# State space and expert layer kernel: fifteen weighted row additions move from VectorE to TensorE, ten held items move behind the first weighted block

## The chip, the cores and the metric

The kernel runs on one core of one Trainium2 chip. The metric is the device time of one execution in microseconds (us); three runs of the kernel before gave 1796.65, 1800.41 and 1805.96, so the median is 1800.41 us. The core has TensorE (PE in the profile, its weight loads are PEld), VectorE (DVE), ScalarE (ACT), GpSimd (POOL, which here issues the gathers) and SyncE (SP, which issues the block loads), each with its own instruction stream, and 16 DMA engines that all queues share. The engines meet through semaphores alone.

## The reference

One layer of a streaming encoder over 512 prompt rows (four tiles of 128 tokens) and 32 sample rows (tile 4), all in float32:

```
h = x + W_out[ concat( shortconv_group(xn), ssd_group(xn) ) ]      # xn = RMSNorm(x)
h = h + CrossAttn(RMSNorm(h), memory K/V)                          # 4 heads, 256 memory rows
h = h + PEER(RMSNorm(h))                                           # 8 heads, top 16 of 16384 experts
y = RMSNorm(h)

# ssd_group, chunk by chunk: decay matrix, two products, state update
y_diag = einsum('bclsg,bclsgh,bcsghp->bclghp', CB, Lm, xdt)
# PEER, per token: 8 heads x 16 experts
hid = gelu( einsum('td,thkd->thk', xb, u_tab[eidx]) )
out = einsum('thk,thkd->td', gate * hid, v_tab[eidx])
```

The last line is what the change touches: a token's output is a sum of 128 rows of `v_tab`, each times a weight of that token.

## The kernel before

**Tiling.** The five token tiles go in two groups: group 0 is tiles 0 and 1, group 1 is tiles 2, 3 and 4. Group 0 passes all dense stages first (input products, convolutions, the state space chain, attention, the expert queries), then group 1. The experts of tiles 1 and 2 are computed densely: all 128 blocks of 128 experts go through TensorE, `lk(b)` multiplying block b of `u_tab` with the tokens (8 matmuls) and `vd(b)` multiplying the weighted result with block b of `v_tab` (4 matmuls, accumulated over all blocks in PSUM banks 0 to 3). The experts of tiles 0, 3 and 4 are gathered: 18 steps i of 16 rows s, one row per token, 0.52 MB for each (i, s) and table.

**Gathered rows.** `("d", i, s)` is a dot product on VectorE of the gathered row of `u_tab` with the token (L1785). After 16 of them ScalarE computes the Gelu (`("ge", i)`, L1328) and VectorE the weights (L1792). `("v", i, s)` then adds weight times gathered row of `v_tab` to the tile (`scalar_tensor_tensor`, L1806). GpSimd issues the gathers in the order u(i, s), v(i-1, s) into rings of four buffers each; a gather waits until the use four before it is done (`u_used`, `v_added`).

**The order.** `plan()` writes one list, `PLAN`, of all work items. Each engine walks through the same list and issues its own part of each item, in order. In the dense stages of group 1 the items of gathered steps 0 to 5 stand between the dense items, placed by a planner with estimated costs. The state space chain of group 1 (the items `s1`, `s2`, `s2b`, `s3`, `s3b`, `s4` of tiles 2, 3, 4, with `z` and `o` projections between them) is such a stage. In it `s2(t)` is on TensorE eight small matmuls (L949), on ScalarE the Relu of their result (L1246), an Exp (L1249) and a small Exp (L1251). `s3(t)` is a product with the state (L962), one with the decay matrix (L969) and one that updates the state (L975). `s4(t)` normalizes the chunk: Square and Sqrt on ScalarE (L1168, L1169), a scaling on VectorE (L1646) and transposes on TensorE (L851), which VectorE drains (L1429).

**PSUM.** There are eight banks. Every TensorE result of the dense stages is a job, job n uses bank n % 8 and waits until job n-8 has been drained.

**The tail.** Before the block loop 22 `lk` are done ahead, with one-hot matmuls `gb` of tile 2 (L1106) between the first of them. The items that the planner took out of the gathered steps 3 to 6 (`late_slots`) are merged with these: the last 22 with `lk(15)` to `lk(21)`. Then VectorE computes `w(0)` to `w(3)` (the weighted hidden values of a block, two instructions each, L1866 and L1867), and the loop goes `w(b+3)`, some gathered items, `vd(b)`, `lk(b+22)`. A buffer of four blocks holds the `w` results, so `w(b)` waits for `vd(b-4)`. The gathered items left over are spread over the blocks in equal shares, at half the share in the last 22 blocks, where there is no `lk` any more. The result of tile t leaves after the last block.

Of the kernel before, what the change touches and what calls it, by code (L numbers as in the profile page):

```python
# [12 lines left out]
P = 128  # L13
# [78 lines left out]
def dense(g):  # L92
# [28 lines left out]
    s += [("o", g, q, t) for q in range(4) for t in TG[g] if ("o", g, q, t) not in s]  # L121

    s += [("norm", 1, t) for t in TG[g]] + kv[10:12]
    if g == 0:
# [75 lines left out]
def plan():  # L200
# [64 lines left out]
    g0 += [("gb", 2, n - 2), ("gb", 2, n - 1)]  # L265
    out += merged(g0, late_slots[4:-22]) + merged(ahead[15:], late_slots[-22:])

    one, two = slots.index(("d", PH + 1, 0)), slots.index(("d", PH + 3, 0))
    extra = merged([x for pair in range(PH // 2) for x in rt(3, pair)] + soft(3), slots[:one])
    extra += merged(rt(NP, 0) + soft(NP), slots[one:two]) + slots[two:]  # L270
    pace = lambda x: dve_us(x) if x[0] in ("d", "v", "final") else 0.0
    work = lambda b: 2 * min(b, NBLK - HRING) + max(0, b - NBLK + HRING)
    total, used, nlk = sum(pace(x) for x in extra), 0.0, HRING
# [85 lines left out]
JOBS = [j for seg in PLAN for j in jobs_of(seg)]  # L359
SEQN = {k: n for n, (k, _) in enumerate(JOBS)}  # L360
OWNER = dict(JOBS)
ORD = {}
# [52 lines left out]
def build_program(nc, a, o):  # L415
    ctx = ExitStack()
    with ctx:
# [133 lines left out]
        OHF = take_(2 * OH_TOK * 2 * P)  # L551
        OH = [cut(OHF, k * OH_TOK * 2 * P, OH_TOK, 2, P) for k in range(2)] + [ar(off, OH_TOK, 2, P) for off in (10752, 12488, 13512)]
        HID, GH, WT = take_(2, TOPK), take_(2, TOPK), take_(2, TOPK)
        assert g_[0] <= 5960, g_[0]
# [23 lines left out]
        ublk_in, vblk_in = [sem(f"ublk_in{r}") for r in range(SR)], [sem(f"vblk_in{r}") for r in range(SR)]  # L578
        lk_done, h_done, wr_done, vd_done = map(sem, "lk_done h_done wr_done vd_done".split())
        xd_done, oh_done, oh_used, g_out, closed = map(sem, "xd_done oh_done oh_used g_out closed".split())  # L580
        hot_done, tt_done, tt_out, fold_done = map(sem, "hot_done tt_done tt_out fold_done".split())
# [21 lines left out]
        def bank_of(key):  # L603
            return PSB[:, SEQN[key] % NB, :]

# [225 lines left out]
        def _(pe):  # L831
            def open_job(key):
                n = SEQN[key]
                if n >= NB:
                    wait_drained(pe, JOBS[n - NB][0])
                return bank_of(key)
# [237 lines left out]
            def settle():  # L1074


                if not settled:
                    for key, _ in JOBS[-NB:]:
                        wait_drained(pe, key)
                    settled.append(True)  # L1080
# [42 lines left out]
            def vd(b):  # L1123
# [17 lines left out]
            does = {"const": const, "state": state, "turn": turn, "memn": memn, "in": in_, "dt": dt, "z": z, "oc": oc, "kv": kv, "kt": kt,  # L1141
                    "s1": s1, "s2": s2, "s3": s3, "s4": s4, "ho": ho, "o": o_, "q": q_, "a1": a1, "a2p": a2p, "a2": a2, "mo": mo,
                    "sk": sk, "pq": pq, "sc": sc, "lk": lk, "tt": tt, "gb": gb, "vd": vd, "fold": fold}
            for seg in PLAN:
# [5 lines left out]
        def _(act):  # L1150
# [201 lines left out]
            def gb(t, n):  # L1352
# [22 lines left out]
                if at + OH_TOK == CH_TOK and c < NSP:  # L1375
                    if small:
                        act.wait_ge(g_out, k + 1)
                    else:
                        act.wait_ge(ev["A"], ORD[("gb", t, n)] + 1)
                    act.dma_start(spill[:, :, c, :].rearrange("k p x -> p k x"),  # L1380
                                  STG[r].rearrange("p (k i) x -> p k (i x)", i=GRP)).then_inc(gs_out[r], 16)

            def leave(t):
                n = rows(t)
                if t in CLOSED:
                    act.wait_ge(closed, CLOSED.index(t) + 1)
                else:
                    act.wait_ge(v_added, (step_of(t, PH - 1) + 1) * TOPK)
                root_mean_square(("leave", t), XN[0:n, t, :], X[0:n, t, :], n, D)

            for row in SMALL_ROWS[:4]:
# [4 lines left out]
                    "ho": ho, "kt": kt, "q": q_, "a1": a1, "a2p": a2p, "a2": a2, "sk": sk, "pq": pq, "sc": sc,  # L1396
                    "keep_x": keep_x, "sme": soft_exp, "ge": gelu, "lk": lk, "oh": oh, "gb": gb, "leave": leave}
            for seg in PLAN:
# [5 lines left out]
        def _(dve):  # L1404
# [427 lines left out]
            def oh(t, n):  # L1832
                d = DENSE.index(t)
                m, c = d * P // OH_TOK + n, n * OH_TOK
                if n == 0 and d == 0:
                    wait_drained(dve, ("tt", 1))
                if n == 0 and d == 1:
                    dve.wait_ge(tt_out, 1)
# [40 lines left out]
            def final(t):  # L1879
# [7 lines left out]
                    "kt": kt, "s1": s1, "s2": s2, "s3": s3, "s4": s4, "o": residual("o"), "a1": a1, "mo": residual("mo"),  # L1887
                    "rt": route, "smd": soft_sum, "d": dot, "v": weighted, "s2b": s2b, "s3b": s3b, "tt": tt, "fold": fold, "oh": oh, "w": w, "close": close,
                    "final": final}
# [33 lines left out]
```

## Time and profile before

| | |
|---|---|
| median of three runs | 1800.41 us |
| lowest, highest | 1796.65, 1805.96 us |
| the profiled execution | 1802.75 us, of which the span is 1801.0 us |
| PE busy | 1678.7 us (93%) |
| PEld busy | 1247.4 us (69%) |
| DVE busy | 1221.1 us (68%) |
| POOL busy | 705.3 us (39%) |
| ACT busy | 366.4 us (20%) |
| moved by DMA | 552.63 MB, mean 307 GB/s |

All times below are from the start of this span. A TensorE instruction on float32 shows as two records, so "x16" of L865 is one projection of eight matmuls, and "x8" of L1128 is one `vd` of four. The granted TensorE clock has two levels, 2.4 GHz (1.00 in the tables) and 1.2 GHz (0.50); a mean between them says how long either held.

### The profile page before, as it was taken

To read this page: it belongs to the slowest core of one execution; us is meant where nothing else is said; L and a number is where in the kernel's file an instruction comes from. 1 tells how busy PE (TensorE), PEld (TensorE's weight loads), DVE (VectorE), ACT (ScalarE), POOL (GpSimd) and SP (SyncE) were. 2 spreads that over 40 slices of the span, in tenths; PEclk is the share of its full clock that TensorE was granted. 3 is DMA by queue.
4 is the path that set the end of the run, shared out by engine and by line. 5 is a ranking of instruction groups with operands and counts; after the bars stand their busy time and mean duration, and the time that the engine had idled before them with its cause. 6 is when DMAs were issued, how large, how long until landed. Compare 5 with 4: busy or idle time off the path is not lost. (4 is left out here: it accounts for less than half of the span.)

```text
span 1801.0 us, 20020 instructions
## 1 busy us (share of the span) xinstructions
PE 1678.7 (93%) x7088; PEld 1247.4 (69%) x7088; DVE 1221.1 (68%) x2626; ACT 366.4 (20%) x910; POOL 705.3 (39%) x601
## 2 busy tenths in 40 slices
PE   7998999999778888899887999999999999999997
PEld 6887888878655677788885666666666666666633
DVE  2352111799688768898987999777666666666675
ACT  1141123111330244642760001101000000000101
POOL 0000000234134438640765555456544444644542
PEclk9999999999878999899998999999999999999999
DMA  6523434789246959995999999999999999999996
GB/s 195 179 93 117 164 117 141 253 271 352 82 140 211 364 175 363 336 345 169 359 318 380 403 407 409 409 409 409 406 408 408 407 409 410 393 410 410 409 376 260
DMA packets 227983, 552.63 MB, mean 307 GB/s; under 512 B 16989, under 2 KB 114957, under 8 KB 227885
## 3 DMA queue, kind: packets, MB, share of 16 engines
q0 software_dynamic: 82944, 302.03, 43.8%
q1 hardware_dynamic: 122180, 237.78, 36.2%
q10 hardware_dynamic: 22760, 11.55, 2.2%
q8 instruction: 57, 0.93, 0.2%
q14 instruction: 42, 0.34, 0.1%
HBM read 534.22 MB, written 16.42 MB: 306 GB/s over the span
## 5 line engine op out<-in xcount | busy, mean ns | idle before, releaser
L809 POOL DMA_INDIRECT M<-in_u_tab,IDX x288 | 342.1, 1188 | 715.9 <-DVE PEER L1785 345.9
L816 POOL DMA_INDIRECT M<-in_v_tab,IDX x288 | 359.2, 1247 | 352.7 <-DVE X L1806 273.7
L1128 PE MATMUL PSB<-M,HST 128*128 128x512 f32 x1024 | 461.6, 596 | 14.8 <-DVE HST L1867 9.9
L1120 PE MATMUL PSB<-XN,M 128*128 128x256 f32 x2048 | 466.4, 382 | 4.9 <-DMA M<-in_u_blocks 3.9
L1120 PEld LDWEIGHTS PSB<-XN,M 128*128 128x128 f32 x2048 | 391.5, 192 | 104.6 <-issue 55.4
L1785 DVE CUSTOM_DVE_ANT_0 M<-M,XN 128x1024 f32<-128x1024 f32 x288 | 351.4, 1221 | 132.8 <-DMA M<-in_u_tab,IDX 120.1
L1806 DVE SCALAR_TENSOR_TENSOR X<-M,PEER,X 128x1024 f32<-128x1024 f32 x256 | 328.1, 1282 | 98.3 <-DMA M<-in_v_tab,IDX 88.3
L1128 PEld LDWEIGHTS PSB<-M,HST 128*128 128x128 f32 x1024 | 195.0, 191 | 218.4 <-issue 201.6
L858 PE MATMUL PSB<-M 128*128 128x256 f32 (+1 forms) x1408 | 327.8, 393 | 9.2 <-DVE M L1429 6.7
L858 PEld LDWEIGHTS PSB<-M 128*128 128x128 f32 x1408 | 266.0, 190 | 64.0 <-DVE M L1429 7.5
L865 PE MATMUL PSB<-M 128*128 128x256 f32 (+1 forms) x1056 | 247.9, 395 | 4.0 <-DMA M<-in_w_out 1.8
L865 PEld LDWEIGHTS PSB<-M 128*128 128x128 f32 (+1 forms) x1056 | 194.8, 187 | 48.9 <-issue 2.4
L1341 ACT ACTIVATE M<-PSB 128x256 f32<-128x256 f32 x128 | 48.7, 381 | 672.1 <-PE PSB L1120 529.8
L1654 DVE TENSOR_TENSOR X<-PSB,X 128x256 f32<-128x256 f32 (+1 forms) x40 | 16.7, 418 | 69.6 <-PE PSB L865 69.6
L1806 DVE SCALAR_TENSOR_TENSOR XN<-M,PEER,XN 128x1024 f32<-128x1024 f32 x31 | 39.8, 1284 | 20.6 <-DMA M<-in_v_tab,IDX 20.3
L1349 ACT ACTIVATE PEER<-PEER 128x128 f32<-128x128 f32 x152 | 48.0, 390 | 28.2 <-DVE PEER L1852 23.1
L1106 PE MATMUL PSB<-PEER 128*128 128x128 f32 x304 | 43.8, 297 | 5.0 <-ACT PEER L1349 2.8
L1852 DVE TENSOR_TENSOR PEER<-iota,PEER 128x1024 f32<-128x1024 f32 x38 | 46.0, 1220 | 3.2 <-PE PSB L1106 1.7
L1106 PEld LDWEIGHTS PSB<-PEER 128*128 128x128 f32 x304 | 41.0, 209 | 8.2 <-ACT M L1370 3.1
L1866 DVE TENSOR_TENSOR HST<-M 128x176 f32<-128x176 f32 x128 | 43.1, 336 | 1.4 <-PE PSB L1128 1.4
L851 PE MATMUL PSB<-ident,M 128*128 128x128 f32 (+1 forms) x160 | 21.3, 281 | 24.0 <-DVE M L1646 19.8
L1168 ACT ACTIVATE XN<-X 128x1024 f32<-128x1024 f32 (+1 forms) x19 | 20.0, 1050 | 114.6 <-DVE X L1654 69.9
(223 smaller groups left out, 1110.5 us busy)
## 6 DMA issues: line engine op xcount, KB each, us to landing
M<-in_u_blocks SPq DMA_DIRECT2D x128, 512.0 KB
M<-in_v_tab SPq DMA_DIRECT2D x128, 512.0 KB
M<-in_w_in SPq DMA_DIRECT2D x24, 1024.0 KB
M<-in_w_pq SPq DMA_DIRECT2D x16, 1024.0 KB
gate_spill<-M ACTq DMA_DIRECT2D x11, 1024.0 KB, 17.0
M<-gate_spill SPq DMA_DIRECT2D x16, 704.0 KB
M<-in_w_out SPq DMA_DIRECT2D x8, 1024.0 KB
M<-in_w_mq SPq DMA_DIRECT2D x8, 1024.0 KB
```

Of the source, the lines that this page charges most:

```text
L809: pool.indirect_dma_start(out=UA[:, s % RR, :], out_offset=None, in_=utab, in_offset=bass.IndirectOffsetOnAxis(ap=IDX[:, n:n + 1], axis=0) ...
L816: pool.indirect_dma_start(out=VA[:, s % RR, :], out_offset=None, in_=vtab, in_offset=bass.IndirectOffsetOnAxis(ap=IDX[:, n:n + 1], axis=0) ...
L858: last = pe.matmul(b[:, 0:n], w[:, c, half * P:(half + 1) * P], src[:, c, :], start=(c == 0), stop=(c == DC - 1))
L865: last = pe.matmul(b[0:n, 0:BW], lhs(c), w[:, c, :], start=(c == 0), stop=(c == DC - 1))
L1106: last = pe.matmul(bank[:, j * P:(j + 1) * P], hot_buffer(t, n)[:, j, 1, :], hot_buffer(t, n)[:, j, 0, :], start=True, stop=True)
L1120: last = pe.matmul(PSB[:, 4 + b % 2, 0:2 * P], UBLK[:, b % SR, c, :], XN[:, 1:3, c * P:(c + 1) * P], start=(c == 0), stop=(c == DC - 1))
L1128: last = pe.matmul(PSB[:, 2 * t + hf, :], WR[:, b % WRING, t * P:(t + 1) * P], VBLK[:, b % SR, hf * 512:(hf + 1) * 512], start=(b == 0), s ...
L1341: act.activation(HR[:, b % HRING, :], PSB[:, 4 + b % 2, 0:2 * P], ACT.Gelu).then_inc(h_done, 1)
L1349: last = act.activation(first, first, ACT.Copy, scale=TT[:, d, 2, c + j:c + j + 1])
L1785: dve.tensor_tensor_reduce(u, u, XN[:, t, :], 1.0, 0.0, ALU.mult, ALU.add, HID[:, par, s:s + 1]).then_inc(u_used, 1)
L1806: dve.scalar_tensor_tensor(out=acc, in0=row, scalar=w, in1=acc, op0=ALU.mult, op1=ALU.add).then_inc(v_added, 1)
L1852: dve.tensor_tensor(hot, bc(iota[:, :].unsqueeze(1).unsqueeze(1), whole), bc(keys.unsqueeze(3), whole), ALU.is_equal).then_inc(hot_done, 1)
```

## The change

First, in the stretch from `s1` of tile 2 to a new item `("sums",)`, which stands ahead of the attention norms of group 1, the fifteen additions `v` of (0, 10) to (1, 8) leave VectorE. For each of them ScalarE builds a diagonal matrix of the weights (Copy of the identity, scaled by the weight of each partition, into a ring of eight), and TensorE multiplies this diagonal with the gathered row, 512 columns at a time, into PSUM banks 6 and 7, where the fifteen products add up. `sums` on VectorE adds both banks to the tile. In this stretch the other jobs use banks 0 to 5 only. The memory of the diagonals is that of the one-hot matrices, which come into use later.

Second, of the 22 late items that were merged with `lk(15)` to `lk(21)` twelve stay there. The last ten (five `d`, five `v`) go to the front of the gathered items of the block loop.

```
@@ dense(g)
+    s += [("sums",)] * g
     s += [("norm", 1, t) for t in TG[g]] + kv[10:12]
@@ plan()
-    out += merged(g0, late_slots[4:-22]) + merged(ahead[15:], late_slots[-22:])
+    out += merged(g0, late_slots[4:-22]) + merged(ahead[15:], late_slots[-22:-10])
...
+    extra = late_slots[-10:] + extra
@@ after PLAN
+SPAN = range(PLAN.index(("s1", TG[1][0])), PLAN.index(("sums",)) + 1)
+ON_PE = [s[1:] for n, s in enumerate(PLAN) if s[0] == "v" and n in SPAN]
+def banks():
+    at, before, last, turn = {}, {}, {}, 0
+    for n, seg in enumerate(PLAN):
+        for key, _ in jobs_of(seg):
+            if n in SPAN and turn % NB >= NB - 2:
+                turn += NB - turn % NB
+            at[key], before[key] = turn % NB, last.get(turn % NB)
+            last[turn % NB] = key
+            turn += 1
...
@@ TensorE
+            def add(i, s):
+                if (i, s) not in ON_PE:
+                    return
+                n, k = i * TOPK + s, ON_PE.index((i, s))
+                if k == 0:
+                    for key in AHEAD_OF_SUMS:
+                        wait_drained(pe, key)
+                    pe.wait_ge(v_added, n)
+                ring_in(pe, va_in, i, s)
+                pe.wait_ge(diag_done, k + 1)
+                for hf in range(2):
+                    last = pe.matmul(PSB[:, NB - 2 + hf, :], DIAG[k % 8], VA[:, s % RR, hf * 512:(hf + 1) * 512],
+                                     start=(k == 0), stop=(k == len(ON_PE) - 1))
+                last.then_inc(v_added, 1)
@@ ScalarE
+            def add(i, s):
+                if (i, s) not in ON_PE:
+                    return
+                k = ON_PE.index((i, s))
+                act.wait_ge(w_done, i + 1)
+                if k >= 8:
+                    act.wait_ge(v_added, i * TOPK + s - 7)
+                act.activation(DIAG[k % 8], ident[:, :], ACT.Copy, scale=WT[:, i % 2, s:s + 1]).then_inc(diag_done, 1)
@@ VectorE
             def add(i, s):
                 t, par, n = step_tile(i), i % 2, i * TOPK + s
+                if (i, s) in ON_PE:
+                    return
...
+            def sums():
+                dve.wait_ge(v_added, ON_PE[-1][0] * TOPK + ON_PE[-1][1] + 1)
+                for hf in range(2):
+                    x = X[:, 0, hf * 512:(hf + 1) * 512]
+                    last = dve.tensor_tensor(x, PSB[:, NB - 2 + hf, :], x, ALU.add)
+                last.then_inc(sums_out, 1)
+                dve.wait_ge(sums_out, 1)
```

What the new list does to the engines' own orders is seen at three places. The line numbers of the changed kernel differ: its L894, L978, L991 are L865, L949, L962 of before, its L1295 to L1297 are L1249 to L1251, its L1268 is L1222, and its L1932 and L1933 are L1866 and L1867.

TensorE in the chain of group 1, from `s2` of tile 2 (L949) on, before; L865 with 32 rows is `z` of tile 4, L962 to L975 is `s3(2)`:

```order
L949 MATMUL PSB<-EARLY,M 128x128 x8
L865 MATMUL PSB<-M 32x256 x8
L962 MATMUL PSB<-HST,M 128x256 x2
L969 MATMUL PSB<-M 128x64 x8
L975 MATMUL PSB<-M 128x256 x2
```

The same place in the changed kernel, L1176 being a product with a diagonal:

```order
L978 MATMUL PSB<-EARLY,M 128x128 x8
L1176 MATMUL PSB<-M,PEER 128x512 x2
L894 MATMUL PSB<-M 32x256 x8
L991 MATMUL PSB<-HST,M 128x256 x2
L998 MATMUL PSB<-M 128x64 x8
```

One product, that of (0, 10), has come between `s2(2)` and the `z` projection that followed it at once.

ScalarE at the same item and up to the norm of the next chunk, changed kernel, from the Exp of `s2(3)` on (L1436 builds a diagonal, L1268 is the Silu of `z`, L1214 and L1215 are Square and Sqrt of `s4(2)`):

```order
L1295 ACT_TABLE_LOAD
L1295 ACTIVATE M<-M 128x1024
L1297 ACTIVATE EARLY<-EARLY 128x24
L1436 ACTIVATE PEER<-ident,PEER 128x128 x2
L1268 ACT_TABLE_LOAD
L1268 ACTIVATE M<-PSB 32x256
L1214 ACTIVATE M,SS<-M 128x512
L1215 ACT_TABLE_LOAD
L1215 ACTIVATE SS<-SS,EPSC 128x1
```

The two diagonals stand behind both Exps of `s2(3)`, and the Silu of `z`, which waits for TensorE, stands ahead of the norm of `s4(2)` as it did before.

VectorE ahead of `w(0)`, changed kernel (L1840 is the dot product L1785 of before, two records each, and L1863 the addition L1806 of before):

```order
L1840 ISA M,PEER<-M,XN 128x1024
L1840 ISA PEER 128x1
L1863 SCALAR_TENSOR_TENSOR X<-M,PEER,X 128x1024
L1932 TENSOR_TENSOR HST<-M 128x176
L1933 TENSOR_TENSOR HST<-M 128x80
```

Ahead of this place stand five dot products and five additions fewer than before. They come after `w(3)`, and with them in the loop the gathered items of all later blocks move back by up to ten items.

## Rows read from the trace of the kernel before

**Rows 1.** Busy time of each engine by stretch, with clock and DMA share

```profile
core 0: us, PE busy (x) PEld busy (x) DVE busy (x) ACT busy (x) POOL busy (x), PEclk, DMA share, GB/s
472.00:592.00 120.00, 93.00 (x418) 68.83 (x418) 93.58 (x242) 31.11 (x72) 38.94 (x31) 0.84 0.51 171
939.00:975.00 36.00, 22.56 (x92) 18.62 (x90) 21.46 (x27) 2.30 (x6) 22.07 (x20) 0.85 1.02 408
975.00:1715.00 740.00, 739.67 (x2560) 487.60 (x2561) 531.54 (x1048) 55.89 (x133) 387.00 (x343) 1.00 1.02 405
```

**Rows 2.** Timeline of TensorE in the chain: start, us, line, idle before and releaser

```profile
480.52 3.64 PE L865 MATMUL PSB<-M 128*32 128x256 f32 x16
...
488.81 2.94 PE L969 MATMUL PSB<-M 128*128 128x64 f32 x16 [3.58 <-issue]
...
508.35 1.12 PE L851 MATMUL PSB<-ident,M 128*128 128x128 f32 x4 [6.36 <-DVE M L1646]
...
528.21 10.00 PE L865 MATMUL PSB<-M 128*128 128x256 f32 x32
541.25 1.11 PE L851 MATMUL PSB<-ident,M 128*128 128x128 f32 x4 [3.04 <-DVE M L1646]
543.15 5.91 PE L865 MATMUL PSB<-M 128*128 128x256 f32 x16 [0.78 <-DVE M L1429]
...
564.54 0.55 PE L851 MATMUL PSB<-ident,M 32*128 32x32 f32 x4 [4.89 <-DVE M L1646]
...
579.46 10.74 PE L865 MATMUL PSB<-M 128*128 128x256 f32 x48 [1.75 <-DMA M<-in_w_out]
591.97 2.58 PE L851 MATMUL PSB<-ident,XN 128*128 128x128 f32 x24 [1.77 <-DVE XN L1457]
```

**Rows 3.** Timeline of ScalarE: ends of s2, the norm of s4, four copies of 128x128

```profile
484.37 0.21 ACT L1251 ACTIVATE EARLY<-EARLY 128x24 f32<-128x24 f32 x1
...
502.19 0.21 ACT L1251 ACTIVATE EARLY<-EARLY 128x24 f32<-128x24 f32 x1
...
503.99 0.61 ACT L1168 ACTIVATE M<-M 128x512 f32<-128x512 f32 x1
...
504.71 1.28 ACT L1169 ACT_TABLE_LOAD   x1
506.00 0.29 ACT L1169 ACTIVATE SS<-SS,EPSC 128x1 f32<-128x1 f32 x1
...
530.79 0.20 ACT L1251 ACTIVATE EARLY<-EARLY 128x24 f32<-128x24 f32 x1
...
631.13 1.28 ACT L1349 ACTIVATE PEER<-PEER 128x128 f32<-128x128 f32 x4 [1.78 <-DVE PEER L1852]
```

**Rows 4.** Timeline of VectorE: one of the additions, in the chain

```profile
501.17 1.28 DVE L1806 SCALAR_TENSOR_TENSOR X<-M,PEER,X 128x1024 f32<-128x1024 f32 x1
```

**Rows 5.** Timeline of TensorE around the first block

```profile
948.82 16.64 PE L1120 MATMUL PSB<-XN,M 128*128 128x256 f32 x64 [3.90 <-DMA M<-in_u_blocks]
975.33 6.54 PE L1128 MATMUL PSB<-M,HST 128*128 128x512 f32 x8 [9.87 <-DVE HST L1867]
...
1005.82 3.60 PE L1128 MATMUL PSB<-M,HST 128*128 128x512 f32 x8
...
1694.49 3.60 PE L1128 MATMUL PSB<-M,HST 128*128 128x512 f32 x8
1697.92 3.62 PE L1120 MATMUL PSB<-XN,M 128*128 128x256 f32 x16
```

**Rows 6.** Timeline of VectorE: first of the ten items, w(0), w(4), w(104)

```profile
956.85 1.23 DVE L1785 CUSTOM_DVE_ANT_0 M<-M,XN 128x1024 f32<-128x1024 f32 x1
...
974.95 0.23 DVE L1867 TENSOR_TENSOR HST<-M 128x80 f32<-128x80 f32 x1
...
984.56 0.23 DVE L1867 TENSOR_TENSOR HST<-M 128x80 f32<-128x80 f32 x1
...
1686.08 0.23 DVE L1867 TENSOR_TENSOR HST<-M 128x80 f32<-128x80 f32 x1
```

More of the change, by code:

```diff
@@ L360 @@
 SEQN = {k: n for n, (k, _) in enumerate(JOBS)}
+SPAN = range(PLAN.index(("s1", TG[1][0])), PLAN.index(("sums",)) + 1)
[9 more added lines that the diff above has]
+            turn += 1
+        if n == SPAN[0]:
+            held = [last[NB - 2], last[NB - 1]]
+        if n == SPAN[-1]:
+            last[NB - 2] = last[NB - 1] = "sums"
+    return at, before, held, [last[b] for b in range(NB)]
+BANK, BEFORE, AHEAD_OF_SUMS, AT_LAST = banks()
 OWNER = dict(JOBS)
@@ L552, in build_program @@
         OH = [cut(OHF, k * OH_TOK * 2 * P, OH_TOK, 2, P) for k in range(2)] + [ar(off, OH_TOK, 2, P) for off in (10752, 12488, 13512)]
+        DIAG = [cut(OHF, k * P, P) for k in range(8)]
         HID, GH, WT = take_(2, TOPK), take_(2, TOPK), take_(2, TOPK)
@@ L579, in build_program @@
         lk_done, h_done, wr_done, vd_done = map(sem, "lk_done h_done wr_done vd_done".split())
+        diag_done, sums_out = sem("diag_done"), sem("sums_out")
         xd_done, oh_done, oh_used, g_out, closed = map(sem, "xd_done oh_done oh_used g_out closed".split())
@@ L603, in bank_of @@
         def bank_of(key):
-            return PSB[:, SEQN[key] % NB, :]
+            return PSB[:, BANK[key], :]
         def bc(ap, shape):
@@ L832, in open_job @@
             def open_job(key):
-                n = SEQN[key]
-                if n >= NB:
-                    wait_drained(pe, JOBS[n - NB][0])
+                before = BEFORE[key]
+                if before == "sums":
+                    pe.wait_ge(sums_out, 1)
+                elif before:
+                    wait_drained(pe, before)
                 return bank_of(key)
@@ L1077, in settle @@
                 if not settled:
-                    for key, _ in JOBS[-NB:]:
+                    for key in AT_LAST:
                         wait_drained(pe, key)
@@ L1142, in _ @@
                     "s1": s1, "s2": s2, "s3": s3, "s4": s4, "ho": ho, "o": o_, "q": q_, "a1": a1, "a2p": a2p, "a2": a2, "mo": mo,
-                    "sk": sk, "pq": pq, "sc": sc, "lk": lk, "tt": tt, "gb": gb, "vd": vd, "fold": fold}
+                    "sk": sk, "pq": pq, "sc": sc, "lk": lk, "tt": tt, "gb": gb, "vd": vd, "v": add, "fold": fold}
             for seg in PLAN:
@@ L1396, in _ @@
                     "ho": ho, "kt": kt, "q": q_, "a1": a1, "a2p": a2p, "a2": a2, "sk": sk, "pq": pq, "sc": sc,
-                    "keep_x": keep_x, "sme": soft_exp, "ge": gelu, "lk": lk, "oh": oh, "gb": gb, "leave": leave}
+                    "keep_x": keep_x, "sme": soft_exp, "ge": gelu, "lk": lk, "oh": oh, "gb": gb, "v": add, "leave": leave}
             for seg in PLAN:
@@ L1836, in oh @@
                     wait_drained(dve, ("tt", 1))
+                    dve.wait_ge(v_added, ON_PE[-1][0] * TOPK + ON_PE[-1][1] + 1)
                 if n == 0 and d == 1:
@@ L1887, in _ @@
                     "kt": kt, "s1": s1, "s2": s2, "s3": s3, "s4": s4, "o": residual("o"), "a1": a1, "mo": residual("mo"),
-                    "rt": route, "smd": soft_sum, "d": dot, "v": weighted, "s2b": s2b, "s3b": s3b, "tt": tt, "fold": fold, "oh": oh, "w": w, "close": close,
+                    "rt": route, "smd": soft_sum, "d": dot, "v": weighted, "sums": sums, "s2b": s2b, "s3b": s3b, "tt": tt, "fold": fold, "oh": oh, "w": w, "close": close,
                     "final": final}
```

## The prediction

> **What bounds the kernel now.** I read the table by stretches first, then the timelines of the engines at the two places that the change touches. From 975 to 1715 us TensorE is busy for 739.67 of 740 us at the full clock [rows 1], so there the sum of its instructions is the time, and any shift at the start of that stretch reaches the end unless something else becomes late in it. The chain of group 1 is different: in the 120 us from 472 to 592 TensorE is busy for 93.0 us and VectorE for 93.58 us, the DMA engines for half the time, and the mean granted clock is 0.84 [rows 1]. Neither engine is full; they wait for one another. TensorE's 27 us of idle time sit at a few points: 6.36, 3.04 and 4.89 us ahead of the transposes of `s4`, and 3.58 us ahead of the first L969 [rows 2]. There VectorE is the one it waits for, and VectorE is late partly because of additions of 1.28 us each [rows 4]. The second place is the start of the block loop: TensorE ends its run of `lk` at 965.5 us, idles 9.87 us for L1867, and then does the first `vd` at half clock, 6.54 us in place of 3.60 [rows 5]. VectorE is late there because of the gathered rows ahead of `w(0)`, the DMA engines being full (408 GB/s, share 1.02) [rows 1].
>
> **The first part, what it takes and adds.** It takes 15 x 1.28 = 19 us from VectorE [rows 4]. It adds 30 matmuls of 128x512. A `vd` is four of that shape, and the next `lk` starts 3.43 us after it (1694.49 to 1697.92; its row says 3.60, the pipelined end included [rows 5]), so two cost 1.72 us at full clock and 15 x 1.72 = 25.7 us go to TensorE; at half clock a pair would be 3.3 us (6.54 / 2). ScalarE gets 15 copies of 128x128; four such are 1.28 us [rows 3], so 0.32 each, 5 us in all on an engine that is 26% busy there. `sums` is two additions of 512 columns from PSUM; half the width of an addition each, so I take 1.3 us, on the path to the norms that follow.
>
> If all the products fell into the 27 us in which TensorE is idle, they would cost nothing. They don't, by position. Each engine takes its part in list order, so TensorE stops at a product until the diagonal is there, and the diagonal stands on ScalarE behind whatever the list has ahead of it. I walk through the chain with the rows of before, at full clock for what is added:
>
> First stop, (0, 10), right behind `s2(2)`. TensorE is free at 480.5 [rows 2]. ScalarE ends the last Exp of `s2(2)` at 484.6 [rows 3], so the diagonal is there at 484.9 and TensorE has idled 4.4 us that it spent on `z` before. With the product TensorE is 6.1 us later (486.6); of these the 3.58 us that it waited ahead of L969 [rows 2] are taken up, so L969 starts 2.6 us later than its 488.81.
>
> Second stop, (0, 11) and (0, 12), behind `s2(3)`. Before, TensorE was done with `z` at 502.0 (508.35 less the wait of 6.36 [rows 2]) and so with `s2(3)` at 498.4. With the shift it is free at 501.0, ScalarE at 502.40 + 2.6 = 505.0 [rows 3]; another 4.3 us of waiting. Two products to 508.7, `z` to 512.3. Now comes what the list order makes of it: the Silu of this `z` stands on ScalarE ahead of the norm of `s4(2)`, so Square, table load and Sqrt, 2.3 us from 503.99 to 506.29 [rows 3], which ran beside `z` and the idle time before, start only at 512.7. With 1 us for VectorE's two small instructions (an estimate) the transposes start at 516.0 in place of 508.35 [rows 2]: 7.7 late. Up to the next L969 VectorE sets the pace and has one addition less: 6.5 late.
>
> Third stop, (0, 14), (0, 15) and then (1, 0). `s2(4)` ends 6.5 late at 534.7, ScalarE at 531.0 + 6.5 = 537.5 [rows 3], 3 us of waiting; two products to 541.2, one `o` projection to 544.8. The diagonal of (1, 0) needs the weights of step 1, which VectorE computes after the residual of this `o` and two dot products (estimates: 0.4 + 2.4 + 0.2, a dot product taken as long as an addition), so it is there at 548.2: 3.3 us of waiting again. Product, second `o` (which ran back to back with the first), residual, norm: transposes at about 554.7 in place of 541.25 [rows 2], 13.5 late. The norm of `s4(3)` also stands behind that diagonal on ScalarE, but is done in time.
>
> From there on diagonals are ready. The `o` projection at 543.15 took 5.91 us at half clock [rows 2] and I take 3.6, the products (1, 1), (1, 2), (1, 3) cost 5.2 and find the 4.89 us of idle time [rows 2]; VectorE, two additions lighter, is not late: 12 late at 564.54. Behind it are projections back to back, so the five products (1, 4) to (1, 8) cost their full 8.6 us, less the 1.75 us wait for a weight block, which has landed by then: 18.7 late. `sums` makes it 20 us at 591.97.
>
> So of 19 us saved on VectorE next to nothing is left, since each of the places where VectorE was late now has ScalarE or TensorE itself late. The two ends for this term: 0 us (all products hidden) and 25.7 + 1.3 + 4 = 31 us (no product hidden, the waits on ScalarE on top, and VectorE's saving only covering the rest). Half clock is not in the walk for the added work. Rows at half clock cost before 10.00 in place of 7.2 and 5.91 in place of 3.6 [rows 2]; the stops leave about 23 us idle in place of 27, in gaps of the same size, so I expect the same kind of loss and add 1 us only, since these losses fall partly into waits. **First part: 21 us later.** Six banks in place of eight: I followed every job to the one six before it; all had been drained by then in the rows of before, so nothing.
>
> The Trainium skill (TensorE: Matmul & The Clock Gate, Architectural detail) says that ScalarE and VectorE have strictly first-in first-out queues while TensorE may pull weight loads ahead. This speaks against the change at the three stops; if a diagonal could overtake the Exps, the sum would lose the first stop's 2.6 us and most of the second's wait. No row here shows an overtaking.
>
> A table load costs 1.28 us and its successor starts at once [rows 3]. The Trainium skill (ScalarE: Activation LUTs, What ACT_TABLE_LOAD costs) gives about 2.66 us with a drain for each switch, and says under Table sets that Copy is in every set. By the latter the diagonals need no load, and the row of the copies in [rows 3] stands behind a Gelu without one; by the former the second stop would be 1.4 us longer than in my walk, which the rows don't bear out.
>
> **The second part.** Without the ten items VectorE reaches `w(0)` at 956.85 in place of 974.7 [rows 6], before TensorE is through with its `lk` at 965.5 [rows 5]. So `vd(0)` starts 9.8 us earlier, and if the clock holds, the first `vd` takes 3.4 in place of 6.5 us: 9.8 to 12.9 us at the head of the full stretch. What is late next: the ten rows, 5.2 MB, are gathered in the loop, which at 408 GB/s is 12.8 us of full DMA engines. The margin is read from when `w(b)` ends and `vd(b)` starts: at block 4 984.8 against 1005.82, 21 us; at block 104 1686.3 against 1694.49, 8.2 us [rows 5, 6]. It shrank by 13 us over a hundred blocks because the gathers (share 1.02 throughout [rows 1]) are slower than the list wants them. With TensorE up to 12.9 us earlier and almost all the ten rows made up for by block 104, the margin there would be 8.2 - 12.9 + 0.5 = -4, and less still towards the last `lk`; so TensorE waits for 4 to 9 us of it. **Second part: 4 to 9 us earlier**, I take 5, since the bytes from 939 us to the end are the same as before and the engines that move them were already full.
>
> Sum: 1800.4 + 21 - 5 = **1816 us** against the median; the profiled execution (1802.75, span 1801.0) would go to 1818.
>
> **Rivals.** (a) The products find their gaps: the stops exist but ScalarE is early enough, or the chain's lateness is made up later, so that the first part costs 0 to 6 us. For it: 27 us idle against 25.7 us added. Against: the order of both lists at the stops. It gives 1800.4 + 0 - 5 = 1795, up to 1806. (b) On the faster side, the clock: with TensorE filled in the chain it stays at 2.4 GHz. The mean of 0.84 over 120 us [rows 1] means 38 us at half clock, and the two rows above lost 2.8 and 2.3 us to it; with the shorter ones I estimate 10 us in all, of which 8 could return. Together with a head of the loop at full clock and DMA engines that keep up, this gives 1800.4 + 0 - 8 - 11 = 1781. It decides if the products close the gaps at the stops. The Trainium skill states such a rule (same page, The HAM clock gate: the default state is throttled and activity releases it); the rows agree that the half clock lies around the idle times, but the three stops keep idle times of 3 to 4.4 us. (c) Worse than my walk: the stops bring the half clock onto the products (3.3 in place of 1.72 for a third of them, 8 us), and the tail gives nothing back: 1800.4 + 30 - 2 = 1828.
>
> **How the numbers follow.** My forecast has a chance of 0.6, with 1807 to 1824 as its own range; (a) 0.2, (b) 0.08, (c) 0.12. The range to hold the time eight times in ten goes from 1795 to 1829. About 0.5%, 9 us, is what a measurement of this kernel can tell from no change. Faster than 1791: all of (b) and a small part of (a), 0.1. Between 1791 and 1809: most of (a) and the low end of the forecast, 0.25. Slower: 0.65.
>
> **What would show it.** In the changed profile the products' line should wait for ScalarE's diagonals (L1436) at three to four places with 3 to 4.5 us each; the transposes of tiles 2, 3 and 4 should start near 516, 555 and 576; the norms' transposes near 612; the stretch from there to the first `vd` should be as long as before less 10 to 13 us; and in the last third of the loop TensorE should wait for L1933 or gathered rows. The forecast is wrong if the products start right behind `s2`, if the stretch 472 to 592 grows by less than 10 us, or if the loop from the first `vd` to the last is no longer than before.

## The result, and the profile after

The changed kernel takes 1827.47 us (median, 1822.38 to 1831.64) against 1799.45 for the kernel before on the same chip: a ratio of 1.0148, interval 1.0118 to 1.0177, 28 us slower. The forecast was 1816, so the sign and the wide range (1795 to 1829) were right, the size was 12 us short, and the time lies above the forecast's own range of 1807 to 1824. The profiled execution of after is the shortest of its four (1822.38, span 1820.6), and stands 19.6 us above that of before. What follows explains these 19.6 us; the rest is scatter between executions that one profile can't show.

I matched TensorE's items one by one in both traces. How much later than before each is:

```
ahead of the chain, nothing changed there yet    +2.6
first transposes of the norms behind the chain  +29.9   chain           +27.3  (forecast +20)
last run of lk ahead of the loop                +20.3   in between       -9.7  (not forecast)
second item of the loop                          +2.2   head of loop    -18.0  (forecast -9.8 to -12.9)
end                                             +19.6   loop            +17.4  (forecast +4 to +9)
```

The chain of group 1 in TensorE's timeline, kernel after (start, us, line, idle before and releaser; L1176 is a product, L1436 a diagonal, L880 the transposes). It answers to [rows 2]:

```profile
487.58 2.83 PE L1176 MATMUL PSB<-M,PEER 128*128 128x512 f32 x4 [4.43 <-ACT PEER L1436]
490.33 4.41 PE L894 MATMUL PSB<-M 128*32 128x256 f32 x16
...
495.64 1.89 PE L998 MATMUL PSB<-M 128*128 128x64 f32 x16
...
509.13 5.30 PE L1176 MATMUL PSB<-M,PEER 128*128 128x512 f32 x8 [4.16 <-ACT PEER L1436]
514.36 3.64 PE L894 MATMUL PSB<-M 128*32 128x256 f32 x16
521.40 0.66 PE L880 MATMUL PSB<-ident,M 128*128 128x128 f32 x4 [3.40 <-DVE M L1701]
...
541.87 5.99 PE L1176 MATMUL PSB<-M,PEER 128*128 128x512 f32 x8 [3.16 <-ACT PEER L1436]
547.70 3.62 PE L894 MATMUL PSB<-M 128*128 128x256 f32 x16
554.73 3.75 PE L1176 MATMUL PSB<-M,PEER 128*128 128x512 f32 x4 [3.41 <-ACT PEER L1436]
558.27 4.58 PE L894 MATMUL PSB<-M 128*128 128x256 f32 x16
563.95 0.66 PE L880 MATMUL PSB<-ident,M 128*128 128x128 f32 x4 [1.11 <-DVE M L1701]
564.45 1.88 PE L1176 MATMUL PSB<-M,PEER 128*128 128x512 f32 x4
...
584.89 0.43 PE L880 MATMUL PSB<-ident,M 32*128 32x32 f32 x4 [1.09 <-DVE M L1701]
```

All four stops of the forecast are there, 4.43, 4.16, 3.16 and 3.41 us where it had 4.4, 4.3, 3 and 3.3. But four of these five rows of products (x4 is one product, x8 two) ran wholly or in part at half clock: 2.83, 5.30, 5.99 and 3.75 us, where at full clock one product is 1.88 (the last row) and two are 3.60 (the same shape in `vd` [rows 5]). The group of all products on after's page (count, then busy us and mean ns, then idle time ahead):

```profile
L1176 PE MATMUL PSB<-M,PEER 128*128 128x512 f32 x60 | 37.5, 766 | 16.1 <-ACT PEER L1436 16.1
```

Fifteen products took 37.5 us, 2.5 each, and TensorE stopped 16.1 us ahead of them, the small fifth stop of 0.96 us included.

The whole chain, from `s2(2)` on TensorE to the first transposes of the norms, columns as in [rows 1], first before, then after:

```profile
478.65:591.97 113.32, 86.33 (x390) 62.76 (x388) 92.37 (x239) 30.22 (x70) 38.91 (x31) 0.85 0.54 181
```

```profile
481.20:621.91 140.71, 111.42 (x450) 68.87 (x449) 76.34 (x226) 35.41 (x87) 34.15 (x31) 0.89 0.48 157
```

TensorE is busy for 25.1 us more and idle for 2.3 us more (29.3 against 27.0). Of its 111.4 us the products are 37.5, so all the other work of the chain took 73.9 us where it took 86.3 before. Half clock did not become longer: by the mean clocks it held for 34 us before (2 x 0.15 x 113.3) and for 31 us after (2 x 0.11 x 140.7). It moved from the other work onto the products.

ScalarE at the first two stops and at the norm of `s4(2)`, kernel after, against [rows 3]:

```profile
486.93 0.21 ACT L1297 ACTIVATE EARLY<-EARLY 128x24 f32<-128x24 f32 x1
487.05 0.39 ACT L1436 ACTIVATE PEER<-ident,PEER 128x128 f32<-128x128 f32 x1
...
508.48 0.21 ACT L1297 ACTIVATE EARLY<-EARLY 128x24 f32<-128x24 f32 x1
508.60 0.68 ACT L1436 ACTIVATE PEER<-ident,PEER 128x128 f32<-128x128 f32 x2
...
518.04 0.37 ACT L1268 ACTIVATE M<-PSB 32x256 f32<-32x256 f32 x1 [7.46 <-PE PSB L894]
518.32 0.61 ACT L1214 ACTIVATE M<-M 128x512 f32<-128x512 f32 x1
```

Each diagonal starts right behind the Exp and costs 0.3 to 0.4 us: the price of a stop is the diagonal's place in the list, not its work. Behind it ScalarE idles 7.46 us for the held-up `z`, and only then comes to the norm, as the walk had it.

TensorE at the start of the loop, kernel after, against [rows 5]:

```profile
966.28 14.40 PE L1149 MATMUL PSB<-XN,M 128*128 128x256 f32 x64 [1.11 <-DMA M<-in_u_blocks]
980.52 3.60 PE L1157 MATMUL PSB<-M,HST 128*128 128x512 f32 x8
983.96 3.62 PE L1149 MATMUL PSB<-XN,M 128*128 128x256 f32 x16
```

The 9.87 us of idle time are gone and the first `vd` is at full clock. Also gone are 2.8 us of the wait for the u block (3.90 before) and 2.2 us of the `lk` run (16.64 before). With 2.9 from the first `vd` that is 17.8 of the 18 us.

Where the loop gives it back: every later row of TensorE with idle time of over 1 us and a releaser other than the block loads of v_tab, kernel after, one by one:

```profile
1357.49 3.72 PE L1149 MATMUL PSB<-XN,M 128*128 128x256 f32 x16 [1.49 <-ACT M L1387]
...
1497.18 3.72 PE L1149 MATMUL PSB<-XN,M 128*128 128x256 f32 x16 [1.47 <-ACT M L1387]
...
1564.09 5.21 PE L1149 MATMUL PSB<-XN,M 128*128 128x256 f32 x16 [4.67 <-ACT M L1387]
...
1732.12 3.67 PE L1157 MATMUL PSB<-M,HST 128*128 128x512 f32 x8 [1.02 <-DVE HST L1933]
...
1803.78 3.62 PE L1184 MATMUL PSB<-XN,stk 128*32 128x512 f32 x4 [4.29 <-DVE XN L1863]
```

At the first three and the last of these places the kernel falls behind before by 1.8, 2.0, 6.4 and 6.2 us, 16.4 of the 17.4. ScalarE and VectorE at the third, kernel after:

```profile
1563.55 0.21 ACT L1374 ACTIVATE PEER<-PEER 128x16 f32<-128x16 f32 x1 [20.91 <-DVE PEER L1840]
1563.67 0.64 ACT L1387 ACTIVATE M<-PSB 128x256 f32<-128x256 f32 x2
```

```profile
1562.28 1.22 DVE L1840 CUSTOM_DVE_ANT_0 M<-M,XN 128x1024 f32<-128x1024 f32 x1 [0.72 <-DMA M<-in_u_tab,IDX]
```

ScalarE had stood 20.91 us at the Gelu of a gathered step (L1374, 16 columns), which needs the last of the step's sixteen dot products (L1840), which had waited for its gathered row. The Gelus of two blocks (L1387) were queued behind it, and the next `lk` writes a PSUM bank that they have yet to read. So a late row reaches TensorE through ScalarE's list. The last place is `fold` (L1184), ahead of the last `vd` in TensorE's list: it waits for the last additions of gathered rows.

### The profile page after: what moved, and what is told of

Same layout as the page of the kernel before. It is cut to its first block and busy times, and to the rows that moved or that the text cites. A ratio compares the mean times of both kernels' runs of the same rounds, so it can differ in the third digit from the quotient of the medians.

```text
span 1820.6 us, 20152 instructions
## 1 busy us (share of the span) xinstructions
PE 1698.7 (93%) x7148; PEld 1247.1 (68%) x7148; DVE 1204.5 (66%) x2613; ACT 369.8 (20%) x925; POOL 697.6 (38%) x601
## 5 line engine op out<-in xcount | busy, mean ns | idle before, releaser
L836 POOL DMA_INDIRECT M<-in_u_tab,IDX x288 | 333.5, 1158 | 728.6 <-DVE PEER L1840 360.9
L1840 DVE CUSTOM_DVE_ANT_0 M<-M,XN 128x1024 f32<-128x1024 f32 x288 | 351.0, 1220 | 131.9 <-DMA M<-in_u_tab,IDX 131.0
L1863 DVE SCALAR_TENSOR_TENSOR X<-M,PEER,X 128x1024 f32<-128x1024 f32 x241 | 308.8, 1281 | 94.3 <-DMA M<-in_v_tab,IDX 91.0
L894 PE MATMUL PSB<-M 128*128 128x256 f32 (+1 forms) x1056 | 243.1, 389 | 0.7 <-ACT M L1349 0.7
L894 PEld LDWEIGHTS PSB<-M 128*128 128x128 f32 (+1 forms) x1056 | 191.6, 184 | 51.6 <-issue 12.3
L1387 ACT ACTIVATE M<-PSB 128x256 f32<-128x256 f32 x128 | 48.4, 381 | 604.3 <-PE PSB L1149 591.1
L1709 DVE TENSOR_TENSOR X<-PSB,X 128x256 f32<-128x256 f32 (+1 forms) x40 | 16.7, 419 | 101.8 <-PE PSB L894 101.8
L1863 DVE SCALAR_TENSOR_TENSOR XN<-M,PEER,XN 128x1024 f32<-128x1024 f32 x31 | 39.9, 1286 | 22.9 <-DMA M<-in_v_tab,IDX 22.7
L1395 ACT ACTIVATE PEER<-PEER 128x128 f32<-128x128 f32 x152 | 48.1, 389 | 29.3 <-DVE PEER L1918 28.2
L1176 PE MATMUL PSB<-M,PEER 128*128 128x512 f32 x60 | 37.5, 766 | 16.1 <-ACT PEER L1436 16.1
L1214 ACT ACTIVATE XN<-X 128x1024 f32<-128x1024 f32 (+1 forms) x19 | 20.0, 1052 | 123.7 <-DVE X L1709 77.2
L1932 DVE TENSOR_TENSOR HST<-M 128x176 f32<-128x176 f32 x128 | 43.1, 337 | 2.0 <-PE PSB L1157 1.9
## 6 DMA issues: line engine op xcount, KB each, us to landing
gate_spill<-M ACTq DMA_DIRECT2D x11, 1024.0 KB, 16.4
```

Of the source, the lines that this page charges most:

```text
L836: pool.indirect_dma_start(out=UA[:, s % RR, :], out_offset=None, in_=utab, in_offset=bass.IndirectOffsetOnAxis(ap=IDX[:, n:n + 1], axis=0) ...
L894: last = pe.matmul(b[0:n, 0:BW], lhs(c), w[:, c, :], start=(c == 0), stop=(c == DC - 1))
L1387: act.activation(HR[:, b % HRING, :], PSB[:, 4 + b % 2, 0:2 * P], ACT.Gelu).then_inc(h_done, 1)
L1395: last = act.activation(first, first, ACT.Copy, scale=TT[:, d, 2, c + j:c + j + 1])
L1840: dve.tensor_tensor_reduce(u, u, XN[:, t, :], 1.0, 0.0, ALU.mult, ALU.add, HID[:, par, s:s + 1]).then_inc(u_used, 1)
```

## The experiments

Diffs are against the kernel named. Ratios are against before on the same chip.

**One part alone.** `e1_products` is after without the moved items, `e2_ten_later` is before with them.

```diff
 e1 (against after)
-    out += ... + merged(ahead[15:], late_slots[-22:-10])
+    out += ... + merged(ahead[15:], late_slots[-22:])
-    extra = late_slots[-10:] + extra
 e2 (against before): the same two lines the other way
```

> Only the first part of the change: the fifteen additions of the chain go to TensorE, the ten items stay with the lk of blocks 15 to 21. From the profile of the changed kernel the chain costs 27.5 us by 592 us of before and some 10 us of it are gone by 940 us. If the two parts add up, this kernel is 18 to 20 us slower than before (ratio near 1.011), the wait of TensorE ahead of the first vd (9.9 us before) is there again, and the loop is as long as before. Rival: the ten moved items cost time themselves, then this kernel is clearly faster than the changed one. It is also open whether the 10 us come back by themselves: the shift of TensorE at 940 us should be near 20 us, not 27.

> Only the second part: the kernel before with the ten held items behind the first block. If the DMA engines bound the loop, the first vd starts 16 to 18 us earlier than before, the loop from there to the last vd is 13 to 17 us longer, the margin of w(b) over vd(b) is used up by about block 70 to 100, and the total is 0 to 5 us faster than before. Rival: the loop gives nothing back by itself (its 17 us in the changed kernel came from the other shifts), then this kernel is 12 to 18 us faster (ratio near 0.991).

e1: 1826.83 us, 1.0136 (1.0091 to 1.0181). e2: 1796.57 us, 0.9998 (0.997 to 1.0026). The products are the whole loss, and the second part is worth nothing that can be measured. e1 was expected 18 to 20 us slower and is 27: of the 10 us made up behind the chain in after it makes up 3.6 only. In e1's trace the chain adds 30 us, the stops are those of after, and no item from the second `vd` on loses or gains more than 1.4 us on before: the loop gives back nothing of a later start. In e2's trace the second `vd` is 16.7 us earlier than before and the kernel 6.1 us earlier behind `vd(83)`, after the same stall as in after. TensorE in the loop of e2, every row with idle time up to 1650 us:

```profile
1471.90 3.67 PE L1129 MATMUL PSB<-M,HST 128*128 128x512 f32 x8 [0.56 <-DVE HST L1868]
...
1476.44 3.72 PE L1121 MATMUL PSB<-XN,M 128*128 128x256 f32 x16 [0.86 <-ACT M L1342]
...
1544.21 6.60 PE L1121 MATMUL PSB<-XN,M 128*128 128x256 f32 x16 [5.53 <-ACT M L1342]
```

The time from the start of the last instruction of `w(b)` to `vd(b)`, the margin, shows it coming; it grows again where TensorE has stalled (us, at blocks 8, 24, 40, 56, 72, 88, 104, 112):

```
before  22.0 20.9 19.4 17.3 12.8 10.7  8.4  5.4
after   23.6 17.2  7.4  7.0  3.8 11.5  4.8  2.8
```

**Are full DMA engines why the loop gives it back?** `h0_half_v_blocks` is before with only the first half of each v block loaded (half of the block product is computed on stale data), `h2_half_v_ten_later` is the same with the ten items moved.

```diff
-                sp.dma_start(VBLK[:, b % SR], vblocks[b]).then_inc(vblk_in[b % SR], 16)
+                sp.dma_start(VBLK[:, b % SR, 0:512], vblocks[b][:, 0:512]).then_inc(vblk_in[b % SR], 16)
```

> The kernel before with only the first 512 of 1024 columns of each block of v_tab loaded (the rest of the output of tiles 1 and 2 is made of stale values), so 33.6 MB fewer are moved in the loop; TensorE's and VectorE's instructions are the same. If the full DMA engines eat the margin of w(b) over vd(b), it stays at 20 us or more to the end, and TensorE's waits behind 1708 us (8 us) are gone: total 6 to 9 us less. Rival: VectorE's own work eats the margin, then it shrinks as before.

> The same half loads with the ten items moved (and nothing else of the change). With the DMA engines no longer full the loop should give nothing back: the first vd 16 us earlier and the total 13 to 18 us less than with the half loads alone. Rival (the loop's give back is VectorE's work on ten more items): the total is within 6 us of the half loads alone.

h0: 1795.17 us, 0.9985 (0.9968 to 1.0002). h2: 1784.88 us, 0.9908 (0.9869 to 0.9946), 10.3 us less than h0, where e2 is not to be told from before. Stretches of the loop, columns as in [rows 1], first before, then e2, then h2:

```profile
1400.00:1750.00 350.00, 346.17 (x1164) 220.71 (x1163) 228.53 (x366) 21.99 (x56) 173.59 (x159) 1.00 1.02 404
```

```profile
1400.00:1750.00 350.00, 340.44 (x1120) 214.52 (x1119) 233.92 (x374) 21.28 (x55) 179.50 (x163) 0.99 1.02 403
```

```profile
1400.00:1750.00 350.00, 350.00 (x1163) 220.90 (x1162) 226.68 (x370) 21.38 (x54) 194.43 (x163) 1.00 0.97 363
```

At 363 GB/s TensorE doesn't stop once, and its lead over before is 10.7 us at the second `vd` and still so at block 100. At 403 GB/s with a share of 1.02 it idles. h2 keeps what the shorter head brought, 11.6 us over h0 in the traces (I had expected 13 to 18); e2 pays it back. So it is the bytes that the loop has to move that make it give back, and not VectorE's work on the ten items, which h2 has too. h0's own gain was smaller than expected: before has some 5 us of waits for v blocks, at its end only.

**Waits or work?** `p0_narrow_products` is e1 with products of 8 columns (the rest of these sums is left out); `r0_no_additions` is before with the chain's fifteen additions narrowed to 8 columns and given to nobody.

```diff
 p0 (against e1)
-                    last = pe.matmul(PSB[:, NB - 2 + hf, :], DIAG[k % 8], VA[:, s % RR, hf * 512:(hf + 1) * 512],
+                    last = pe.matmul(PSB[:, NB - 2 + hf, 0:8], DIAG[k % 8], VA[:, s % RR, hf * 512:hf * 512 + 8],
 r0 (against before; GONE lists the v items of the chain)
+                if (i, s) in GONE:
+                    acc, row = acc[:, 0:8], row[:, 0:8]
```

> First part alone, each product narrowed from 512 to 8 columns per matmul (the result of tile 0 lacks fifteen rows): TensorE still waits for the diagonals at the same places and still loads the diagonal as weights, but has next to no work with them. It splits the first part's 27 us in the chain into waits and work. Theory: waits and list order (the norm's Square behind the late z) give about 10 to 13 us, the products' own time the rest, so the chain is 10 to 14 us late and the total 6 to 12 us above the kernel before. Rival (waits are harmless): within 3 us of the kernel before.

> The kernel before with the fifteen additions of the chain narrowed from 1024 to 8 columns (tile 0 lacks their sum) and nothing given to TensorE: what VectorE's relief of some 17 us is worth at the most. From the timeline, TensorE waits 6.4, 3.0 and 4.9 us for VectorE ahead of the three s4, of which 1.3 (ScalarE's norm is next), 3 and 3.5 us can go, plus a little at s3: the chain 6 to 10 us shorter, total ratio near 0.995. Rival (TensorE's idle time is all VectorE's): 15 us or more shorter.

r0: 1790.15 us, 0.995 (0.9933 to 0.9966). p0: 1811.04 us, 1.0059 (1.0039 to 1.0078). A narrowed addition still takes 0.22 us, so 15.9 of the 19 us of additions are off VectorE. That brings 10 us and no more; after it TensorE still waits there, for VectorE's longer work (9.0 us at three transposes). TensorE's line of products in e1 and then in p0, groups of the chain:

```profile
L1175 PE MATMUL PSB<-M,PEER 128*128 128x512 f32 x60 | 36.2, 741 | 16.1 <-ACT PEER L1435 16.1
```

```profile
L1175 PE MATMUL PSB<-M,PEER 128*128 128x8 f32 x60 | 10.3, 286 | 16.4 <-ACT PEER L1435 16.4
```

The waits are equal (16.1 and 16.4) and the products 26 us shorter, yet the time falls by 14 to 16 us only. So of e1's 27 us over before about half is the products' length, and the other 10 to 11 us remain with products of 10.3 us. The latter hold the stops and the norms queued behind them, less what VectorE saves. Narrow products aren't free, and they move the half clock again: the chain in e1, then in p0.

```profile
488.52:630.18 141.66, 112.39 (x450) 70.20 (x449) 76.34 (x226) 35.39 (x87) 34.33 (x31) 0.87 0.48 155
```

```profile
487.37:612.46 125.09, 93.36 (x450) 69.19 (x448) 76.17 (x226) 35.28 (x87) 34.11 (x31) 0.86 0.52 175
```

Without its products e1's TensorE is busy for 76.2 us and p0's for 83.0. So part of what the products lose goes to the work beside them, and the split is a rough one.

**Mend the stops.** `e3_early_diag` is e1, with the six diagonals of step 0 built by ScalarE ahead of `s1(2)`, their weights being known by then.

```diff
+EARLY_DIAG = [x for x in ON_PE if x[0] == 0]
             for seg in PLAN:
+                if seg == PLAN[SPAN[0]]:
+                    for key in EARLY_DIAG:
+                        add(*key)
+                if seg[0] == "v" and seg[1:] in EARLY_DIAG:
+                    continue
```

> First part alone, but ScalarE builds the six diagonals of step 0 before the chain starts, in place of behind the Exps of s2; TensorE's order is that of the changed kernel. Theory (the waits for ScalarE make the chain late): three of the four waits of 3 to 4.4 us on the diagonals vanish, the chain is 12 to 16 us late in place of 27, the total 8 to 14 us faster than with the first part alone. Rival (it is TensorE's added 25.7 us and the half clock): the idle time only moves to the next wait on VectorE, the total is within 4 us of the first part alone.

e3: 1805.04 us, 1.004 (1.0015 to 1.0066), 22 us less than e1. The group of products in the chain, e3:

```profile
L1176 PE MATMUL PSB<-M,PEER 128*128 128x512 f32 x60 | 33.4, 691 | 4.4 <-ACT PEER L1436 4.4
```

Three stops (12 us) are gone and the one on step 1's weights (3.4) stays. The chain adds 8.0 us in place of 30. The same stretch as above, e3:

```profile
480.76:602.12 121.36, 103.12 (x451) 64.65 (x449) 76.31 (x226) 33.52 (x81) 35.76 (x31) 0.96 0.56 182
```

Against e1 that is 11.0 us less idle time and 9.3 us less busy time for the same instructions, the mean clock being 0.96 in place of 0.87. The gain was larger than the 8 to 14 us expected, because I had priced the waits and not the half clock that goes with them.

**Put the products into the gaps.** `e4_in_gaps` is e3 where TensorE holds the products back and does them just ahead of L969 in `s3` and of the transposes of `s4`, where it waits for VectorE anyway. `e5_ten_products` gives the last five, which have no gap, back to VectorE. `e6_ten_products_ten_later` adds the change's second part; `e7_ten_products_four_later` moves four items in place of ten.

```diff
 e4 (against e3)
+            def flush():
+                while held:
+                    product(*held.pop(0))
+            def add(i, s):
+                if (i, s) in ON_PE:
+                    held.append((i, s))
+                    if (i, s) in AT_ONCE:
+                        flush()
 (flush() ahead of L969 in s3 and first in s4; AT_ONCE: the products behind the last s4)
 e5 (against e4)
-ON_PE = [s[1:] for n, s in enumerate(PLAN) if s[0] == "v" and n in SPAN]
+ON_PE = [... and n in SPAN and n < PLAN.index(("s4", NP))]
```

> First part alone with early diagonals, and TensorE does the products of the chain just ahead of its waits: ahead of L969 in s3 and of the transposes of s4, where it was idle for 3.6, 6.4, 2.5, 3.0 and 4.9 us before. The last five products stay among the projections. Theory: the ten products cost next to nothing, VectorE's relief shows, and the chain is 0 to 8 us late, all of it from the last five products (8.6 us); total 0 to 6 us slower than before. Rival (the added work costs its time wherever it stands): 18 to 26 us late.

> The kernel with products just ahead of TensorE's waits, without the ten moved items, and with ten products in place of fifteen: the last five, which stood among back to back projections, are additions on VectorE again. Theory (a product costs nothing in an idle gap and its full 1.7 us among projections): 8 us faster than with all fifteen, the projections after s4 of tile 4 as long as before, total 5 to 9 us faster than the kernel before (ratio near 0.996). Rival (TensorE's and VectorE's lists catch up with each other after the chain anyway): no difference from the fifteen.

> The same with the ten held items behind the first block as well. By the runs so far the first vd comes 16 us earlier and the loop gives 10 us or more of it back. Theory (DMA engines full in the loop): no more than 4 us faster than without the move, perhaps slower, since the chain's gain starts the loop earlier still. Rival: another 10 us faster.

> Ten products in TensorE's gaps and only four of the held items behind the first block in place of ten. The first vd gains some 7 us in place of 16, the loop gives back 4 us or less of it. If the margin in the loop decides, this is as fast as the version with ten moved (0.9943) within 2 us; if the head decides it lies halfway between that and the version without a move (0.9981).

```
e4  1798.70 us  0.9997 (0.9982 to 1.0013)
e5  1795.70     0.9981 (0.9962 to 1.0)
e6  1788.94     0.9943 (0.992  to 0.9965)
e7  1794.98     0.9971 (0.9955 to 0.9988)
```

The groups of products in the chain, e4, then e5:

```profile
L1187 PE MATMUL PSB<-M,PEER 128*128 128x512 f32 x60 | 28.1, 602 | 1.0 <-ACT PEER L1447 1.0
```

```profile
L1187 PE MATMUL PSB<-M,PEER 128*128 128x512 f32 x40 | 18.4, 597 | 0.0
```

The waits are gone, and a product costs 1.87 us (28.1 / 15) where in after it cost 2.5 (37.5 / 15). The chain in e4:

```profile
478.81:593.49 114.68, 103.39 (x451) 67.21 (x449) 76.08 (x226) 33.56 (x81) 32.75 (x31) 0.96 0.57 193
```

It is 1.4 us longer than before with fifteen products in it. TensorE idles 11.3 us in it, 27.0 before and 29.3 in after, and the mean clock is 0.96 against 0.85 and 0.89. The Trainium skill (TensorE: Matmul & The Clock Gate, The HAM clock gate) says that activity releases the throttle; these rows agree. This is rival (a) with some of (b), and it needed other lists.

e5 was expected 5 to 9 us faster than before and is 2 to 3, with an interval that reaches 1.0; in its trace the chain is 6.7 us shorter than e4's. e6, expected to gain at most 4 us on e5, gains 7.

**The best again.** `e8_best_again` is e6 once more, in more rounds on another chip, with no edit.

> The same kernel as e6_ten_products_ten_later, timed again in five rounds, since it is the one that beats both: ratio 0.992 to 0.997 against the kernel before if the first comparison holds, and 0.998 or more if that was chance.

1794.67 us against 1801.26: 0.9957 (0.9934 to 0.9981). Faster than before by 0.4 to 0.6%, a gain as small as the bound of what can be told here. e6 too gives back in the loop: from 23.3 us ahead of before at the second `vd` to 15.5 behind `vd(83)`, so ten moved items run into the full DMA engines there too. e7, which should have given back 4 us or less, was not better: from 14.1 us ahead it falls to 5.9 behind `vd(92)`, most of it at a wait of 5.19 us for ScalarE's Gelus. Why four moved items cost as much as ten was not looked for.

## Why the prediction was right, and where its sizes were off

- **The three stops and the stop for step 1: right,** in place and within 0.2 us in size. Their order of the lists was the reason for the sign, and e3 and e4 show it by removing them.
- **The chain's length: 7 us too small, and the term that was mis-sized is the idle time.** The products took 37.5 us against 15 x 1.84 = 27.6 in e5's terms, 10 us more than at full clock; rival (c) had put 8 us on just this. But the other work of the chain took 12.4 us less, so the forecast's 1 us for the clock, "the same kind of loss", holds in sum: busy time grew by 25.1 us, forecast 25.7 less 2.3 for one projection plus 1. The idle time was to fall from 27 to about 23 us and is 29.3. The stops are 1 us of this, the fifth one. The rest are small waits that the walk had at nothing or shorter: 1.86 and 2.12 us ahead of `s2` of tiles 3 and 4 (0.22 and 1.33 before), 0.90 ahead of L998, 1.09 ahead of `s4(4)`, 2.69 ahead of the norms (1.77 before). So losses to half clock did fall partly into waits before, as the forecast said, and it missed the other side of that: the TensorE work of tile 3 ahead of `s2(3)` took 2.8 us before and 1.5 after, and the wait behind it grew by 1.6. No run changes the clock alone, so how much of the 7 us is clock and how much is waits for VectorE stays open. It shows in the walk. Less the 2.6 us of ahead, the chain is late by 4.2 at L998 (forecast 2.6), 10.4 at `s4(2)` (7.7), 20.1 at `s4(3)` (13.5), 17.7 at `s4(4)` (12), 27.3 at the norms (20). The largest excess, 3.9 us, is between `s4(2)` and `s4(3)`, where the three rows of products are 2.86, 5.99 and 3.75 us, for 6.9 at full clock, and TensorE idles 10.7 us (7.6 before).
- **Time made up after the chain: missing from the sum,** -9.7 us. The stretch from the chain's end to the last `lk` run, first before, then after:

```profile
591.00:934.00 343.00, 312.25 (x1691) 263.23 (x1692) 291.84 (x568) 170.99 (x451) 174.03 (x112) 0.95 0.86 301
```

```profile
621.90:954.60 332.70, 305.33 (x1694) 257.01 (x1695) 290.81 (x565) 169.13 (x448) 175.82 (x111) 0.97 0.86 304
```

  For the same items TensorE is busy 6.9 us less, at a clock of 0.97 against 0.95, and idle 3.4 us less. So most of it is less work at half clock. Why the clock was better there stays open. Item by item, e3 made up 8.0 us in the same stretch, e4 7.5 and e1 3.6; e2, where the chain was not changed, made up 4.1 too, and two executions of one kernel, e6 and e8, 4.6 and 0.4. So part of it can be scatter. No run was made for it.
- **The head of the loop: right in kind, 5 us too small.** The idle time and the half clock were counted, the shorter wait for the u block and the faster last `lk` run were not.
- **The give-back: right in cause, mis-sized.** The forecast was 4 to 9 us in the last third of the loop, with waits for L1933 or gathered rows. It is 17 us, from `vd(54)` on. The walk made the margin shrink by bytes alone and let TensorE wait for `w(b)`. The rows show an earlier and costlier way, through ScalarE's Gelu of a gathered step and the Gelus behind it, and one at `fold`. Net, the second part is worth 0 and not 5.
- **The forecast's own test** ("wrong if the stretch grows less than 10 us, or the products start right behind `s2`") came out on its side. Rival (b) and, for after, rival (a) fell. The time, 1827, is the 1828 of rival (c), half by its mechanism: the products met the half clock as it said, but the other work got as much back, and the tail brought nothing, as it said, but by gaining 18 us and losing 17.
- **Luck.** The terms were off by 7 (chain), 10 (made up behind it), 5 (head) and 8 to 13 us (loop), and these cancel in part. That the total came within 12 us, and inside the wide range by 1.5, is owed to that too.
- The sum of the profiled execution, 2.6 + 27.3 - 9.7 - 18.0 + 17.4 = 19.6, is 8 us under the difference of the medians. e1's profiled execution was the longest of its four (1834.83) and after's the shortest, so the 12.5 us between their traces are no cost of the second part: by the medians, 27 and 28 us over before, the two kernels are equal.

## What to carry to other kernels

Work that moves from a full engine to an idle one pays only if it lands in that engine's existing waits, with its operands ready: the same fifteen products cost 27 us where the list put them, and nothing where their diagonals came early and they stood just ahead of waits that were there anyway. Price a moved instruction by what is queued ahead of its producer and by the clock that it will meet, not by its busy time. And time won by moving row items into a stretch whose DMA engines are full comes back as waits within it, unless bytes leave it too (e2, e6, e7 against h2). Time won ahead of it with nothing moved in is kept: e5 and r0 came to the second `vd` 9.3 and 11.3 us ahead of before and ended 11.6 and 13.8 ahead.

## What the runs showed that I had not expected

- Executions with the same instructions up to that point differ by up to 8 us ahead of the chain (the first item of the chain is 2.6 us late in after, 8.2 in e1, 2.1 in e3, 0.2 in e4), where no change can be the cause. Shifts have to be taken between two points of the same trace, never from the start.
- A product of 8 columns still costs TensorE 0.69 us for its four records (10.3 / 15) against 2.4 for 512 columns (36.2 / 15): a narrowed matmul is no removed matmul.
- In the loop 6 us can be lost to one row: ScalarE stood 20.91 us at a Gelu of 16 columns, with the work of two blocks behind it.
